# Another mixer for a hybrid decoder step: tokens in the order meta, samples, prompt, the 80-column tile first, norm sums under the z units, the conv half of the output projection early

## The reference

```
h += 0.5 * SwiGLU_1(RMSNorm(h))
p  = RMSNorm(h) @ w_in      # q | k | v | z (4 heads x 128 each) | beta, alpha (4 each) | val, gate (512 each)
qkv = silu(conv4(q|k|v));  q, k = l2norm(q) / sqrt(128), l2norm(k)
o  = gated_delta(q, k, v, exp cumulative gates, beta, state)  # prompt from a zero state, each sample from its own
o  = rmsnorm(o) * o_norm * silu(z)
c  = silu(rmsnorm(conv31(val * sigmoid(gate)) + conv_b) * conv_norm)
h += [o | c] @ w_out
h += 0.5 * SwiGLU_2(RMSNorm(h));  y = RMSNorm(h) * final_norm
```

## Time and profile before

| | us |
|---|---|
| median of 3 timed runs | 1364.58 (1362.32 to 1368.38) |
| span of the profiled execution, first to last instruction | 1358.4 |
| PE busy | 1290.4 (95%) |
| DVE busy | 607.2 (45%) |
| ACT busy | 393.1 (29%) |
| POOL busy | 124.1 (9%) |

### The profile page before, as it was taken

The page is one execution under the profiler, slowest core; times in us unless marked ns, Lnnn a source line. Parts: engine busy times, 40 slices in busy tenths (PEclk is TensorE's granted clock), DMA queues, the critical chain, the costliest instruction groups (busy, mean ns, idle before and its releaser), DMA issues.

```text
span 1358.4 us, 22496 instructions
## 1 busy us (share of the span) xinstructions
PE 1290.4 (95%) x9335; PEld 1252.1 (92%) x9335; DVE 607.2 (45%) x773; ACT 393.1 (29%) x545; POOL 124.1 (9%) x88
## 2 busy tenths in 40 slices
PE   5999999999999999999789998989999999999995
PEld 4999999999999989999678886889999999999994
DVE  5434234332336535674347554644443343423443
ACT  5432122221224423331323313434321222212232
POOL 3000000000002200000234422130000000000011
PEclk9999999999999999999789997899999999999997
DMA  7322222222222222113000000321222222222252
GB/s 229 100 77 80 88 75 83 77 78 81 78 87 95 78 72 69 63 48 109 1 1 1 1 1 29 130 96 49 93 77 94 78 77 88 82 81 86 82 96 72
DMA packets 35977, 101.28 MB, mean 75 GB/s; under 512 B 11856, under 2 KB 12240, under 8 KB 35536
## 3 DMA queue, kind: packets, MB, share of 16 engines
q1 hardware_dynamic: 35776, 98.09, 23.0%
q10 hardware_dynamic: 144, 2.36, 0.5%
HBM read 95.00 MB, written 5.44 MB: 74 GB/s over the span
## 4 chain that ended last, share of the span: by engine, by line
PE 90%; DVE 6%; issue 2%; ACT 2%; DMA 0%; POOL 0%; POOLq 0%; DVEq 0%; SPq 0%; ACTq 0%
PE ps L435 77%; PE ps L509 11%; DVE x_lo L1170 1%; PE ps L489 0%; DMA raw<-weights 0%; DVE h L1550 0%; DVE d_inv_t L1430 0%; DVE d_decay L1368 0%; DVE qkv L1477 0%; DVE qkv L1360 0%; ACT w_hi L844 0%; DVE qkv L1361 0%; PE ps L531 0%; DVE rstd L1176 0%; PE ps L449 0%
## 5 line engine op out<-in xcount | busy, mean ns | idle before, releaser
L435 PE MATMUL ps<-x_hi,w_hi 128*128 128x296 f32 (+1 forms) x1920 | 420.8, 300 | 20.7 <-DVE x_lo L1170 19.7
L435 PE MATMUL ps<-x_lo,w_hi 128*128 128x296 f32 (+1 forms) x1920 | 416.7, 299 | 0.0
L435 PE MATMUL ps<-x_hi,w_lo 128*128 128x296 f32 (+1 forms) x1920 | 415.2, 298 | 0.0
L435 PEld LDWEIGHTS ps<-x_hi,w_hi 128*128 128x128 f32 x1920 | 311.6, 189 | 24.7 <-issue 17.4
L435 PEld LDWEIGHTS ps<-x_lo,w_hi 128*128 128x128 f32 x1920 | 312.4, 189 | 0.0
L435 PEld LDWEIGHTS ps<-x_hi,w_lo 128*128 128x128 f32 x1920 | 311.2, 189 | 0.0
L1165 DVE TENSOR_TENSOR w_lo<-raw,w_hi 128x1024 fp32r<-128x1024 f32 x168 | 205.5, 1224 | 192.3 <-ACT w_hi L844 190.1
L844 ACT CAST w_hi<-raw 128x1024 fp32r<-128x1024 f32 x168 | 175.0, 1042 | 308.1 <-PE ps L435 279.2
L435 PE MATMUL ps<-g_hi,w_hi 128*128 128x296 f32 (+1 forms) x704 | 152.5, 298 | 1.0 <-DVE g_lo L1195 1.0
L435 PE MATMUL ps<-g_lo,w_hi 128*128 128x296 f32 (+1 forms) x704 | 152.0, 297 | 0.0
L435 PE MATMUL ps<-g_hi,w_lo 128*128 128x296 f32 (+1 forms) x704 | 151.4, 296 | 0.0
(11 more groups left out here) (209 smaller groups left out, 996.0 us busy)
## 6 DMA issues: line engine op xcount, KB each, us to landing
raw<-weights SPq DMA_DIRECT2D x168, 512.0 KB, 3.4
h<-x_t SPq DMA_DIRECT2D x2, 1184.0 KB, 5.5
new_state<-S ACTq DMA_DIRECT2D x1, 2304.0 KB, 9.6
y_t<-h SPq DMA_DIRECT2D x8, 288.0 KB, 2.4
S<-states SPq DMA_DIRECT2D x1, 2048.0 KB, 10.2
mask<-masks SPq DMA_DIRECT2D x1, 836.5 KB, 7.9
dft<-dfts SPq DMA_DIRECT2D x1, 741.0 KB, 9.4
c_ext<-hist_c SPq DMA_DIRECT2D x4, 120.0 KB, 7.5
```

The costliest lines, as they stand in the source:

```text
L435: last = nc.tensor.matmul(ps[:, slot if out is None else out, half, 0:w_half], w[:, slot, k, :], x[:, k, a:a + w_half], start=(k == 0 and ...
```

## The change

1. The token order becomes meta, samples, prompt. The tile of 80 columns (16 meta tokens and 64 sample tokens) is now tile 0 with four levels' worth of chain; the tiles of 128 prompt tokens are 1 to 4. Evacuations of the q, k, v units, of val and gate, and of the convolution are cut at the new borders, which adds one instruction for each.
2. The gate sums, the norm sums of all five tiles and the mean squares of the convolution leave the schedule and stand between and behind the z units, with their ACT and DVE parts.
3. `samples` and `final` become `first`, eleven steps behind chain 0. The meta tokens give the prompt's first state (`s_ps`), and each later tile's scan has all its products. The states are spread over eight samples, not nine groups.
4. The SiLU of z, the SiLU of the conv channels and the casts are steps of the schedule. The output projection's input has buffers of its own (xoc, xoh). The conv half (slices 4 to 7) of its units 0 and 1 is done inside the last scan (`out_half`), the o half after it.
5. x_hi and x_lo of the second FFN are made tile by tile behind each output unit.
6. SyncE stores the conv history rows and last_q before the output weights' loads and not at the end.

The diff, cut to its core:

```diff
-TILES = [(128 * t, 128) for t in range(4)] + [(512, 80)]
+TILES = [(0, MAIN)] + [(MAIN + 128 * t, 128) for t in range(4)]
-LEVELS = [7, 7, 7, 7, 4]
+LEVELS = [4, 7, 7, 7, 7]
...
-    out = [("gates", 0, i) for i in range(3)] + merge(prep[0], prep[1])
-    lag1, lag3 = 10, 10
-    out += merge(merge(chain[0], chain[1][:lag1]), tok[0] + tok[1] + prep[2])
-    out += merge(merge(chain[1][lag1:], chain[2][:4]), prep[3])
-    out += merge(merge(chain[2][4:], chain[3][:lag3]), merge(scan[0] + scan[1], prep[4]) + tok[2] + tok[3])
-    out += merge(chain[3][lag3:], merge(chain[4][:4], scan[2]))
-    out += merge(merge(tok[4] + scan[3], chain[4][4:]),
-                 [("samples", hd, 0) for hd in range(H)] + [("conv", c, 0) for c in range(NC_)])
-    out += final[0:2] + [("weights", 0, 0)] + final[2:4] + [("conv", 4, 0)] + final[4:5] + [("weights", 1, 0)] + final[5:]
+    out = merge(prep[0], prep[1])
+    out += merge(merge(chain[0], chain[1][:8]), tok[0] + tok[1] + first[:1] + prep[2])
+    out += merge(chain[1][8:12], first[1:5])
+    out += merge(merge(chain[1][12:], chain[2][:8]), first[5:] + prep[3])
+    out += merge(merge(chain[2][8:], chain[3][:8]), tok[2] + silu + scan[1] + prep[4])
+    out += merge(merge(chain[3][8:], chain[4][:8]), tok[3] + cast + scan[2] + tok[4])
+    out += merge(chain[4][8:-1], heads[:3] + scan[3] + heads[3:] + weights)
+    out += chain[4][-1:] + scan[4]
...
@@ TensorE, after each of the last units i (12 to 15 are z) @@
                 between(i)
+                if i == NQ:
+                    gate_sums()
+                    norm_sums(0, 4, 5)
+                if i == NQ + 1:
+                    norm_sums(1, 4, 5)
+                    conv_means()
+                if i == NQ + 2:
+                    norm_sums(2, 4, 5)
+            norm_sums(3, 4, 5)
+            norm_sums(4, 6, 7)
...
@@ VectorE, the z units @@
+            z_scaled(0)
+            gate_sums()
+            qk_scaled(0)
+            dve.wait_ge(s["facs"], 1)
+            V.tensor_tensor(f_kbg[:], gate["beta"][:], f_cum[:], ALU.mult).then_inc(s["f_ready"], 1)
+            z_scaled(1)
+            qk_scaled(1)
+            dve.wait_ge(c_factor, 2)
+            for i in range(NC_):
+                V.scalar_tensor_tensor(work[:, 4 + i, 0:TOK], work[:, 4 + i, 0:TOK], v("conv_b", i), ssum[:],
+                                       ALU.add, ALU.mult).then_inc(c_scaled, 1)
+            z_scaled(2)
+            qk_scaled(2)
+            z_scaled(3)
+            dve.wait_ge(unit_done, U_OUT)
+            gate_rows(0)
+            gate_rows(1)
+            qk_scaled(3)
...
@@ TensorE, steps of first @@
+                if i == 0:
+                    pe.wait_ge(state_in, 16)
+                    pe.wait_ge(s["ek_ready"], 1)
+                    for hd in range(H):
+                        for gi in range(1, NG):
+                            last = state_products(hd, gi)
+                    last.then_inc(s["ss_ps"], 1)
...
+                if i == 5:
+                    pe.wait_ge(s["osq_ready"], 1)
+                    mm(heads(6, n), ones[:], h4(work[:, 3, :], n)).then_inc(s["on_ps"], 1)
+                if i >= 7:
+                    hd = i - 7
+                    pe.wait_ge(s["vx_ready"], hd + 1)
+                    if hd == 0:
+                        pe.wait_ge(s["o_log"], 1)
+                        pe.wait_ge(s["s_ready"], 1)
+                    else:
+                        pe.wait_ge(s["s4_ready"], hd)
+                    for half in range(2):
+                        last = mm(bank(6 + half), KG[0][0:n, hd, :], VX[hd % 2][:, 512 * half:512 * (half + 1)])
+                    last.then_inc(s["s4_ps"], 1)
...
@@ TensorE, the last scan @@
+                    if t == 4:
+                        out_half(0, 4, 5)
...
+                    if t == 4:
+                        out_half(0, 5, 8)
+                        out_half(1, 4, 8)
...
+            def out_half(j, k0, k1):
+                for k in range(k0, k1):
+                    for r, (w, lo) in enumerate(((w_hi, False), (w_hi, True), (w_lo, False))):
+                        for half in range(2):
+                            a = LATE + half * w_half
+                            x = xoc_lo if lo else xoc_hi
+                            nc.tensor.matmul(ps[:, OUT_SLOT[j], half, 0:w_half], w[:, j, k, :], x[:, k - 4, a:a + w_half],
+                                             start=(k == 4 and r == 0), stop=False, skip_group_check=True)
...
@@ ScalarE, end of the output projection @@
-            prepare(2, None, out_tile, split=False, lo=LATE)
-            act.wait_ge(unit_done, U_FFN2)
-            for k in range(KT):
-                nc.scalar.activation(x_hi[:, k, LATE:], h[:, k, LATE:], ACT.Copy,
-                                     scale=v("ffn2_norm", k)).then_inc(x_hi_ready, 1)
+            prepare(2, "ffn2_norm", out_tile, lo=LATE)
@@ VectorE, the same @@
             for k in range(KT):
-                add_to_h(U_OUT + k, k % 4, k, 1.0, LATE)
+                add_to_h(U_OUT + k, OUT_SLOT[k % 4], k, 1.0, LATE)
                 split_lo(U_OUT + k + 4, k % 4)
-            for k in range(KT):
-                rest_of_x(k, "ffn2_norm", 24, LATE)
+                rest_of_x(k, "ffn2_norm", 16, LATE)
```

More of the change, by code:

```diff
@@ L795, in final, with nothing @@
                     last.then_inc(s["s4_ps"], 1)
-            def weights_split(j, _):
+            def nothing(t, i):
                 pass
-            steps = {"gates": gates, "prep": prep, "tok": tok, "start": start, "level": level, "end": end, "scan": scan,
-                     "conv": conv, "samples": samples, "final": final, "weights": weights_split}
+            steps = {"prep": prep, "tok": tok, "start": start, "level": level, "end": end, "scan": scan, "first": first,
+                     "silu": nothing, "cast": nothing, "heads": nothing, "weights": nothing}
@@ L1107, in weights_split, with nothing @@
             def weights_split(j, _):
                 if j == 0:
-                    act.wait_ge(s["p_ps"][0], LVO[4] - 2 + LEVELS[4] - 1)
+                    act.wait_ge(s["at_ready"], NT)
+                    act.wait_ge(s["att_ready"], NT)
                 split_hi(U_OUT + j, j)
-            steps = {"gates": gates, "prep": prep, "tok": tok, "start": start, "level": level, "end": end, "scan": scan,
-                     "conv": conv, "samples": samples, "final": final, "weights": weights_split}
+            def nothing(t, i):
+                pass
@@ L1114, in _ @@
+            steps = {"prep": prep, "tok": nothing, "start": start, "level": level, "end": end, "scan": scan, "first": first,
+                     "silu": silu, "cast": cast, "heads": lambda t, i: x_heads(t), "weights": weights_split}
             for name, t, i in delta_schedule():
                 steps[name](t, i)
-            act.wait_ge(s["att4_ps"], 1)
-            for i in range(H):
-                act.wait_ge(mix_ready, i + 1)
-                nc.scalar.copy(x_hi[:, i, LATE:], qkv[:, i, LATE:]).then_inc(x_hi_ready, 1)
@@ L1494, in final @@
-            def final(_, i):
-                t, (c0, n) = 4, TILES[4]
-                cols = slice(c0, c0 + n)
-                if i == 1:
+                    dve.wait_ge(s["s_ready"], t)
+                    for hd in range(H):
+                        last = V.scalar_tensor_tensor(S[:, hd, 0, :], S[:, hd, 0, :], f_all[:, t, hd:hd + 1],
+                                                      heads(6, P)[:, hd, :], ALU.mult, ALU.add)
+                    last.then_inc(s["s_ready"], 1)
+                    dve.wait_ge(z_ready, H)
@@ L1509, in final @@
                 if i == 6:
[L1510 to L1517 removed]
+                    normed(0, cols, n)
@@ L1521, in weights_split, with nothing @@
                     dve.wait_ge(s["p_ps"][0], LVO[4] - 2 + LEVELS[4] - 1)
+                    dve.wait_ge(s["p_ps"][1], LVO[3] - 1 + LEVELS[3] - 1)
                 split_lo(U_OUT + j, j)
[L1524 to L1525 removed]
+            def nothing(t, i):
+                pass
+            steps = {"prep": prep, "tok": tok, "start": start, "level": level, "end": end, "scan": scan, "first": first,
+                     "silu": nothing, "cast": cast, "heads": lambda t, i: x_heads(t), "weights": weights_split}
             for name, t, i in delta_schedule():
                 steps[name](t, i)
[L1529 to L1536 removed]
             split_lo(U_OUT + 2, 2)
@@ L1668, in _ @@
+            steps = {"prep": prep, "tok": nothing, "start": start, "level": level, "end": nothing, "scan": nothing,
+                     "first": first, "silu": nothing, "cast": nothing, "heads": nothing, "weights": nothing}
             for name, t, i in delta_schedule():
```

801 lines of the change are left out of this document (430 added, 371 removed).

## The result

The changed kernel takes 1371.24 us (1370.68 to 1374.29) against 1364.58; the ratio is 1.0056, 95% interval 1.0039 to 1.0073. It is slower by a little over half a per cent, where 1343.6 us, 21 us faster, was predicted.

What follows compares the result with a forecast made beforehand. TensorE loses 63 of the mixer's 206.2 us, most winnable at front and tail. From the z units' end, terms sum to 244.0 us against 265.0, 21.0 less: 1364.6 to 1343.6 us, range 1334 to 1353 (chance 0.57).

Steps and rivals of the forecast that it cites:

- The z stretch: z units with the moved sums: 10.9 us of work moved in plus 1 us for alternation, bounds 0 and 6.
- rival 3: Between z units: the norm round is not covered by a z unit; at 13.5 us each, 1371 us; chance 0.07.
- the conv half in the last scan: Mixer's end: 6.4 us of conv slices taken from the output projection cover TensorE's waits in the last scan.
- the second FFN's gap: Behind the output projection: the 4.3 us gap and 1.8 us of slow clock both go, 6.1 less; bounds 3 and 6.1.
- the output projection: Without its first 2.7 us at half clock and the conv halves, 44.8 us remain of 52.6.
- rival 2: Middle of the list: GpSimd and VectorE block each other, some 16 instructions 0.96 us more each, 15 us: 1359; chance 0.09.
- the middle: Mixer's middle: some 80 us of work with two chains at 13% loss, 12 plus 3, 15 us lost; bounds 10 and 22.
- chain 4's lone levels: Mixer's tail: chain 4's last three levels alone, 15.3 us, filled with scan 3 and casts, 4 us lost.
- a table load or two, each up to 0.8: Mixer's middle: table loads, SiLUs, casts, residuals and gating on a queue with a chain's copies; 3 us added for the middle.
- Front, first steps and clock: Mixer's beginning: 13.5 us lost in the front, 7 in the first steps, 4 by the clock after the 16-column run.
- none for the last 40 us before the output projection: Mixer's end, a sign to look for: no half clock in the last 40 us before the output projection.
- Rival 1: Mixer: in-order queues give the loss back, losses stay at 63 us; 15 us more, 1358.9; chance 0.12.

Runs made afterwards that it cites:

- experiment 6: exp. 1's kernel with 11.6 us of GpSimd work left out (state scalings, v_new spreads in two heads; part of the computation missing): 1364.05 us, ratio 1.0000.
- exp. 1: The changed kernel with the table that holds Ln and Exp loaded right after the last SiLU of the conv channels: 1364.78 us, ratio 1.0005.
- exp. 5: exp. 1's kernel with the 64 state products of 16 columns moved right behind chain 0's second start step: 1357.58 us, ratio 0.9956.
- exp. 7: exp. 5's kernel with chains closer together, so chain 1 is alone for two steps, not four, and chain 2 for three, not five: 1351.53 us, ratio 0.9914.
- exp. 10: exp. 7's kernel with the chains one step closer, one lone step less each for chains 1 and 2: 1344.97 us, ratio 0.9865.
- experiment 9: exp. 7's kernel with GpSimd's four state scalings moved from steps 1 to 4 of `first` to steps 5 to 8: 1356.35 us, ratio 0.9953.
- experiment 2: The changed kernel with the run of 64 state products cut into four steps, one per head, spread over chains 0 and 1: 1376.72 us, ratio 1.0074.
- experiments 8: exp. 7's kernel with only 8 of the 64 state products done (part of the computation left out): 1342.33 us, ratio 0.9846.

## Why the prediction was wrong

**Right, shown.** The z stretch (37.4 us for 38.2, no wait of TensorE over 1 us in it; rival 3 is out), the conv half in the last scan (undone: 8.1 us more, term 6.4), the second FFN's gap (5.9 for 6.1), the output projection (44.58 for 44.8), the work (139.4 counted, 139.3 forecast), and no price for GpSimd beside VectorE. VectorE's long forms are there: L1550 takes 1.840 us in the mean, and 1.03 for 80 columns (L1416 before: 1.638 and 2.25); the forms that rival 2 priced are short (experiment 6). The measured 1371.24 is the 1371 of rival 3, but by chance: its waits between z units are not there.

**The step that failed** is the middle: "some 80 us of work with two chains at the present rate of loss (15.4 / 115.3 = 13%)", plus 3. It lost 30.8 of 93.0 us, 33%. Here is the mixer cut at its steps, not at round times: us lost by the same count of matmuls, in after and in four of the experiments (the times in the first column are those of after; the sums agree with those above within half a us):

| stage | after | exp. 1 | exp. 5 | exp. 7 | exp. 10 |
|---|---|---|---|---|---|
| to chain 2's first product (737.8) | 27.3 | 27.3 | 18.4 | 17.2 | 14.4 |
| to the last product of `first` (754.9) | 6.3 | 6.3 | 8.0 | 7.2 | 6.9 |
| to chain 3's first product (775.3) | 8.1 | 8.1 | 6.7 | 5.2 | 1.9 |
| to chain 3's end step (839.4) | 19.2 | 15.1 | 15.5 | 15.4 | 14.9 |
| to the output projection | 16.2 | 10.4 | 15.0 | 11.9 | 11.9 |

A first part of the miss is lone steps. The rate was read from a stretch in which two chains run side by side nearly always, and the list of the change does not keep that up. Chain 2 needs chain 0's buffers, so it starts behind `first`; of its first 8 steps 3 have chain 1 beside them, 5 have nobody. The prediction saw the 4 lone steps of chain 1 and the 6 of chain 4, and priced the rest as paired. The third row is where chain 2 is alone: 8.1 us lost of 20.4, and 1.9 of 16.0 in experiment 10. Taking 6 of the 9 lone steps of chains 1 and 2 away gave 1357.6 to 1345.0, 12.4 us by the ratios (experiments 7 and 10); in the traces 10.5 stand in the first four rows, and 3.1 in the last, where the step order is the same and the clock is not. The price of a lone level was taken as its idle part, 2.4 us; moving the chains showed 3.5.

The larger part is the fourth row, where two chains do run side by side. It lost 19.2 of 64.1 us in after; 4.1 of these went with the table loads, and 15 of 60 us, 25%, are still lost in each experiment of the table; at 13% its 45 us of work would have lost 7. So the rate itself did not carry over to the new lists, paired or not, and why is open. And chain 4's lone levels, priced at 4 us lost, lost 11.0 between chain 3's end and chain 4's (839.4 to 866.2), and 7.7 without the table loads (experiment 1).

**Mis-sized within it: "a table load or two, each up to 0.8".** The trace has 8 in the norm of o and each takes 1.283 us; 7 us by experiment 1. The length stood in the trace of before too, where every load takes 1.283 us; no row gives 0.8. The SiLU steps were costed by their duration alone, not by what they leave loaded.

**Front, first steps and clock, 24.5 forecast, 33.9 lost.** Chain 0's first product came at 677.40, 10 us behind the last z unit for the 12 forecast. Then TensorE stood 5 us for d_kg, because VectorE had the start steps of two chains ahead of it, and that wait was no step of the prediction. The clock was down from 685 to 692, ahead of the 64 products, back for 3 us and down again from 695.5 to 709. The wait isn't all that brings it down: in experiment 5, without it, the clock is down from 685.5 to 699.5. Placing the products into that wait gave 6.7 us (experiment 5). The clock's loss, 4 in the forecast, was by 692.4:710.2 alone 6.6 us. The sign "none for the last 40 us before the output projection" failed too: the clock was at 0.50 from 862.5 to 869.5.

**3.5 us ahead of the z units** lie in code that the change touches with a few short evacuations only. A clock phase is seen there (granted 0.72 in 482 to 488, where before has 1.00, and about 0.86 in 524 to 536), and not in one place of the change. These two phases are nearly the whole of it: 0.28 of 6 us and 0.14 of 12 us are 1.7 each, 3.4 together. In experiment 9, whose trace has none before the z units, these start at 627.40; in experiment 2, which has one, at 628.69. Why they come is open. They stand in most traces of the new kernels and not in the one trace of before, which is of an unusually short run, so they may be a part of what lies between the 10.5 us of the traces and the 6.7 of the medians; that is not shown.

Altogether: 7 (tables), 6.7 (products into the wait) and 12.4 (lone levels) are 26.1 of the 27.6 us by which the medians missed. The split between the last two is less sure than their sum: experiment 5's trace loses 8.9 us less than experiment 1's before chain 2's first product, and 4.6 more in the last row, where nothing was moved. In experiment 10 the mixer loses 21.0 us before 740, 22.1 in 740 to 830 and 6.8 after, 50 in sum; the forecast had 24.5, 15 and 8.5, together 48. So 1345.0 beside the forecast of 1343.6 is partly luck: the middle is still 7 us over, and front and tail are under. Rival 1, losses that stay at 63 through the in-order queues, had the right kind of mechanism and too small a size: 76.9 (its own sum gives 1358.6, not 1358.9).

**Open.** Why the middle of experiment 10 still loses 25% (22.1 of 90 us), where before lost 13% with two chains; TensorE's waits there are many and short (in 740 to 830 4.4 us in 4 for d_inv_t, 2.5 in 2 for qo, 3.1 in 2 for the start of chains). In the front less GpSimd work changed nothing; in the middle nothing was tried, not the offset of the two chains either, which is 8 steps now and was 10 or 4 before. Why the clock falls 3 to 4 us earlier in experiment 7 than in 5 and 10 is open too.

## What to carry to other kernels

A rate of loss belongs to the pairing in which it was measured. Before using it on a new order of steps, write out for each step who runs beside it, and price the lone ones at more than their idle part (3.5 us here, for 2.6 idle of 5.3). Even with the same pairing a rate is a guess for a new order: 13% became 25%. List for each ScalarE instruction that moves which table it needs and which it leaves, and preload the shared one behind the last intruder. Work that waits for little (here 64 small matmuls) belongs where TensorE waits first, not where its result is next needed.

## What the runs showed of the hardware

- In after an Ln and an Exp that follow each other load two tables, 1.283 us each, unless the one with both was loaded explicitly; 8 loads became 1.
- The clock fell behind a pause of TensorE and before the first 16-column matmul, and stayed at 0.50 through 23.7 us in which TensorE was busy without a gap (experiment 2). With 8 of the 64 products it was down from 684.5 to 695, with all 64 from 682 to 699 (experiments 8 and 7).
- One program had two times, 1366 and 1374 to 1380 us, with nothing changed between runs; mean clocks of 0.980 and 0.978 go with the first, 0.966 to 0.972 with the second (experiment 2). What the clock did in the shorter runs is on no trace.
- The same units at the same code start later by the slow phases before them: the z units at 627.40 with none, 628.69 with one, 630.10 with two (experiments 9 and 2, after).
